# Token mixing rounds: GpSimd instead of VectorE makes the low part of one weight unit per round

## The chip, the cores and the metric

The kernel runs on one core of a Trainium2 chip. The metric is the device time of one execution in microseconds (us), and of several executions the median. The core has TensorE (PE in the profile), VectorE (DVE), ScalarE (ACT), GpSimd (POOL) and SyncE (SP), each with its own queue that is worked off in order. They meet at semaphores. TensorE's weight loads are shown as PEld.

## The reference, cut to what matters

Three layers in a row: a mixing layer (a recurrent branch and a sparse attention branch), a feed-forward layer with 16384 experts, and a second block of two attention-like layers. Only the first is touched, and in it the recurrent branch:

```python
p_rw, q, c_kv, iq, ik, iw, gates = _split(xn @ w_in[l], IN_SPLITS)
y_a = _rwkv7_time_mix(p_rw, ...) @ w_branch_rwkv[l]
y_b = _dsa_attention(q, c_kv, iq, ik, iw, ...) @ w_branch_dsa[l]
g_a, g_b = jnp.split(jax.nn.sigmoid(gates), N_BRANCHES, axis=-1)
h = h + (g_a * y_a + g_b * y_b) @ w_out[l]
...
def step(S, inp):            # inside _rwkv7_time_mix, over 256 tokens
    r_t, k_t, v_t, kk_t, a_t, w_t = inp
    sa = jnp.einsum('bhvk,bhk->bhv', S, -kk_t)
    S = (S * w_t[:, :, None, :] + sa[..., None] * (kk_t * a_t)[:, :, None, :]
         + v_t[..., None] * k_t[:, :, None, :])
    return S, jnp.einsum('bhvk,bhk->bhv', S, r_t)
```

Everything is float32. The recurrence of 16 heads of 64 columns isn't walked token by token in the kernel but in chunks, which needs the inverse of a small triangular matrix for each block of 16 tokens.

## The kernel before, in words

**Weights.** All large weights come in one stream, cut into units of 128 x 2048 float32 (1 MB). A unit passes through one of four slots (`SLOTS`), unit u through slot u % 4: SyncE fetches it into `ring`, ScalarE rounds it to `hi_w` in two halves of 1024 columns (`split_hi`, lines 217 and 218), and another engine makes the rest `lo_w` = `ring` - `hi_w` in two halves (`split_lo`, lines 223 and 225; in this part of the kernel VectorE through the local `lo`). TensorE multiplies three times, hi x hi, lo x hi and hi x lo (line 695, in `quarter`), 24 products of 512 columns for a unit, in four quarters. When it is through with unit u, it raises `unit_used`, and SyncE fetches unit u + 4. So VectorE makes the low part of unit u + 3 while TensorE is at about unit u.

**The block that the change touches** runs 92 units (`LASTU`). Each engine has a loop over them, written out at build time, and between units stand the steps of the other work, at fixed places given as unit and quarter (`due`). The engines other than TensorE number their steps one ahead (`U = u + 1`).

**Token mixing rounds.** There are four rounds n = 0 to 3, each 12 units after the one before: half of the heads (8) for half of the tokens (128). Round n starts at unit 35.25 + 12 n (`RB`, `RSTEP`). Of a round these steps matter here, with their distance in units from the start:

- `steps_out`, `steps_in`: the small triangular blocks go out to DRAM and come back as `Lp` (GpSimd issues the second).
- `off_block` (5.25, line 1549) and **`solve`** (6 to 6.5, lines 1557 to 1562), both on VectorE: `solve` is the forward substitution, 15 times a product `terms` <- `Xs`, `Lp` and a sum over it into `Xs`, with a drain between any two. The last raises `X_ready`.
- `steps_back` on GpSimd waits for `X_ready`, writes `Xs` out to `T_dram` and, when that has landed, reads it back as `TC` (lines 1337, 1342).
- `keys_norm` of the next round (lines 1478 to 1489, with a square root on ScalarE at 1268).
- `spread` (10, line 1571) on VectorE makes `TT` from `TC`; the drain behind it (line 1573) raises `TT_sb`.
- `first` (10.25, line 915) on TensorE waits for `TT_sb`; `second` and `third` (lines 924, 931) follow.

In round 0 VectorE has the token shift of other columns in between (`shift`: lines 1460, 1464, 1468, on `prev` and `RKV`); its first step waits for a transfer that GpSimd issues. In round 3 the three parts of `solve` alternate with `turned_y` (line 1634, one input in PSUM), and behind them in VectorE's queue stands `gated(77)` (line 1646), which reads the products of units 76 and 77 from PSUM and so gives TensorE their bank back for the last two quarters of unit 78. GpSimd has nothing in this block but memsets and transfers; further on in the kernel it does make low parts (line 2076).

In VectorE's queue the low part of unit 44, 56, 68 or 80 (slot 0 each time) stands right behind `solve` in rounds 0 to 2, and behind `gated(77)` in round 3.

Of the kernel before, what the change touches and what calls it, by code (L numbers as in the profile page):

```python
# [19 lines left out]
SLOTS = 4  # L20
# [95 lines left out]
def build(nc, dram, consts):  # L116
# [13 lines left out]
    def S(name):  # L130
        if name not in sems:
            sems[name] = nc.alloc_semaphore(name)
        return sems[name]
# [379 lines left out]
    rows = [slice(CH * c, CH * c + CH) for c in range(NCH)]  # L513
    RB, RSTEP, LASTU, DSAU = 35.25, 12, 92, 36
    LMB = (3, 4, 6, 7)

    def due(u, g, o):

# [22 lines left out]
    with nc.Block() as block:  # L541
# [755 lines left out]
        @block.gpsimd  # L1297
        def _(g):
            def shift(m):

                n = WIDTH.get(m, 512)
                src = zs if m == 4 else part_of(m - 5)
                if m == 4:
                    g.wait_ge(S("iq_T"), 1)
                else:
                    g.wait_ge(S("mixed"), m - 4)
                g.memset(prev[0:1, 0, :], 0.0).then_inc(S("prev_zero"), 1)
                g.wait_ge(S("rkv_in"), m - 3)
                g.dma_start(prev[1:P, :, 0:n], src[0:P - 1, :, 0:n]).then_inc(S("prev_in"), 16)
                g.dma_start(prev[0:1, 1, 0:n], src[P - 1:P, 0, 0:n]).then_inc(S("prev_in"), 16)  # L1310

            def gate_out(c):

                g.wait_ge(S("gate_sb"), c + 1)
                g.dma_start(gates[:, :, c * 512:(c + 1) * 512].rearrange("t p f -> p t f"), gst[:]).then_inc(S("gate_out"), 16)

            def steps_in(n):

                g.wait_ge(S("L_out"), 128 * n + 128)
                if n == 0:  # L1320
                    g.wait_ge(S("z_ps"), 1)
                else:
                    g.wait_ge(S("T_out"), 32 * n)
                g.dma_start(Xs[:], consts["unit_x"].rearrange("p (j t) -> p j t", j=8)).then_inc(S("X0_in"), 16)
                for q in range(2):
                    g.dma_start(Lp[64 * q:64 * q + 64], Ld.rearrange("h b s t -> (h b) s t")).then_inc(S("L_in"), 16)

            def clear(ap, name):
                g.memset(ap[0:64, :, 64:P], 0.0)
                g.memset(ap[64:P, :, 0:64], 0.0)  # L1330
                g.drain().then_inc(S(name), 1)

            def steps_back(n):

                g.wait_ge(S("X_ready"), n + 1)
                for q in range(2):
                    g.dma_start(Td.rearrange("h b s t -> (h b) s t")[:, 8 * q:8 * q + 8, :], Xs[64 * q:64 * q + 64])\
                        .then_inc(S("T_out"), 16)
                g.wait_ge(S("T_out"), 32 * n + 32)
                if n:  # L1340
                    g.wait_ge(S("TT_sb"), n)
                g.dma_start(TC[:], Td.rearrange("h b s t -> h (b s) t").rearrange("h r t -> r h t")).then_inc(S("T_in"), 16)

            def mix_out(c):

                g.wait_ge(S("mb_sb"), c + 1)
                g.dma_start(mixed_dram[:, :, c * 512:(c + 1) * 512].rearrange("t p f -> p t f"), part_of(1 + c % 2))\
                    .then_inc(S(f"mb_out{c % 2}"), 16)

            for u in range(LASTU):  # L1350
                m, q = divmod(u, SLOTS)
                if u == 32:
                    g.wait_ge(S("z_ps"), 1)
                    g.memset(zgT2[32:33, 0, :], 1.0)
                    g.memset(zgT2[64:65, 0, :], 1.0)
                    g.memset(zgT2[32:33, 1, :], 0.0)
                    g.drain().then_inc(S("one_row"), 1)
                for n in range(4):
                    if u == math.ceil(RB + RSTEP * n + 3.6):
                        steps_in(n)  # L1360
                        clear(state_of(n, 1), "K_zero")
                    if u == math.ceil(RB + RSTEP * n + 6.5):
                        steps_back(n)
                if q == 3 and 4 <= m <= 10:
                    shift(m)
                if q == 3 and 11 <= m < 19:
                    gate_out(m - 11)
                if u == 46:
                    g.wait_ge(S("scaled"), 7)
                    clear(ST0[:], "ST0_zero")  # L1370
                if u >= WIN and u < WIN + 8 and (u - WIN) % 2:
                    mix_out((u - WIN) // 2)

        @block.vector
        def _(v):
# [286 lines left out]
            for U in range(1, LASTU + 1):  # L1662
                u = U - 1
                m, q = divmod(u, SLOTS)
                if u == 3:
                    norm_c()
                if u in PAIR:
                    maxima(PAIR[u])
                if u >= WIN and (u - WIN) % 2:
                    gated(u)  # L1670
                if u + 3 < LASTU + 2:
                    lo(u + 3)
                if u in (11, 13):
                    scores((u - 11) // 2)
                if u == 12:
                    top(0, 0, 8)
                    penalty(0)
                if 14 <= u < 18:
                    top(1, 2 * (u - 14), 2)
                if u == 18:  # L1680
                    penalty(1)
                if u in PAIR:
                    scale_p(PAIR[u])
                if 5 <= m <= 11 and q < 3:
                    shift(m - 1, q)
                if u == 74:
                    v.wait_ge(S("o_hi"), 2)
                    v.tensor_tensor(lo_x[:, 0:8], oT[:], hi_x[:, 0:8].bitcast(F32), ALU.subtract)
                    v.drain().then_inc(S("o_lo"), 1)
                for g in range(4):  # L1690
                    if (U, g) == (WIN + 9, 2):
                        turned_y(3)
                    for n in due(U, g, -3):
                        keys_norm(n, 0)
                    for n in due(U, g, -2.5):
                        keys_norm(n, 1)
                    for n in due(U, g, 0.5):
                        rates(n)
                    for n in due(U, g, 1.5):
                        prepare(n)  # L1700
                    for n in due(U, g, 2):
                        ends(n)
                    for n in due(U, g, 2.5):
                        turned_k(n)
                    for n in due(U, g, 3):
                        masked(n, range(4))
                    for n in due(U, g, 3.5):
                        masked(n, range(4, 8))
                    for n in due(U, g, 4):
                        bonus(n)  # L1710
                    for n in late_due(U, g, 15.75, 12.75):
                        center(n)
                    for n in late_due(U, g, 16.25, 13.25):
                        finish(n)
                    for n in due(U, g, 5.25):
                        off_block(n)
                    for k in range(3):
                        for n in due(U, g, 6 + k / 4):
                            solve(n, k)
                    for n in due(U, g, 10):  # L1720
                        spread(n)
                    for n in due(U, g, 10.5):
                        copy4(n, one1, 4, "one_ps", "one_v")
                    for n in due(U, g, 10.75):
                        v.wait_ge(S("two_ps"), n + 1)
                        for q in range(4):
                            tt_(one2[:, 2 * q:2 * q + 2].rearrange("p e (a c) -> p a e c", a=2),
                                PS[:, 5 + q // 2, (q % 2) * 256:(q % 2 + 1) * 256].rearrange("p (e a c) -> p a e c", e=2, a=2),
                                EM[:, q].rearrange("p a (e c) -> p a e c", e=2), ALU.add)
                        v.drain().then_inc(S("two_v"), 1)  # L1730
                        fades(n)
                    for n in due(U, g, 11):
                        copy4(n, WU, 4, "W_ps", "W_v")
                    for n in due(U, g, 11.25):
                        moves(n)
                    if U == WIN + 1 and g:
                        turned_y(g - 1)
# [564 lines left out]
    GU, AU, KU, LASTU = 48, 64, 80, 83  # L2302
# [494 lines left out]
    QU, AU, LASTU = 16, 32, 48  # L2797
# [557 lines left out]
```

## Time and profile before

| what | us |
|---|---|
| median of 3 runs | 3724.7 (3722.67 to 3726.25) |
| the profiled execution | 3719.19 |
| its span from first to last instruction | 3717.4 |
| TensorE busy | 3547.2 (95% of the span) |
| VectorE busy | 2148.9 (58%) |
| ScalarE busy | 1740.7 (47%) |
| GpSimd busy | 345.0 (9%) |

The mean granted clock of TensorE is 0.979 of full speed. How to read the rows further down: a timeline row gives start and duration of an instruction in us from the start of the span, then engine, line, operation, `out<-in`, the shapes, and in brackets for how long the engine had been idle before it and what ended that. A duration in a row of VectorE or GpSimd contains the time for which the instruction was started but held up. A q behind an engine's name means its sequencer (a drain, a semaphore or the issue of a transfer).

### The profile page before, as it was taken

The numbers are of one execution on the slowest core, as the hardware profiler recorded it, in microseconds if no ns is written. First come the engines' busy times: TensorE is split into PE (matmuls) and PEld (weight loads), VectorE is DVE, ScalarE is ACT, GpSimd is POOL, SyncE is SP. The second block draws the span as 40 slices with busy tenths as digits, with TensorE's granted clock in tenths as the row PEclk, the third lists the DMA queues.
The fourth block names the chain that finished last, engine by engine and source line by source line (L and its number), as shares of the span: only waits on it lengthen the run. The fifth ranks groups of instructions, "written<-read, shape, count | busy, mean of one in ns | idle before, by whom it ended". The sixth has DMA issues, their size and how long they took to land. (4 is left out here: it accounts for less than half of the span.)

```text
span 3717.4 us, 50884 instructions
## 1 busy us (share of the span) xinstructions
PE 3547.2 (95%) x20442; PEld 3018.0 (81%) x20442; DVE 2148.9 (58%) x2858; ACT 1740.7 (47%) x2595; POOL 345.0 (9%) x217
## 2 busy tenths in 40 slices
PE   7899999988889999999999999998799999999999
PEld 6677777677779999888899998887688887788777
DVE  4676556644545668655544455554678876465454
ACT  4454333323334478544444444444555544444762
POOL 0001000000039910000000000000022210000000
PEclk9999999899999999999999999999899999999999
DMA  5464234344535555555555565555443434455344
GB/s 209 137 209 146 100 135 150 138 182 160 182 136 181 181 173 177 185 214 192 186 210 182 211 252 189 209 189 192 140 141 139 142 132 182 174 192 193 125 148 159
DMA packets 111179, 638.53 MB, mean 172 GB/s; under 512 B 18506, under 2 KB 24426, under 8 KB 38936
## 3 DMA queue, kind: packets, MB, share of 16 engines
q1 hardware_dynamic: 105128, 621.90, 47.0%
q0 software_dynamic: 5296, 13.15, 1.1%
q8 instruction: 115, 1.88, 0.2%
q10 hardware_dynamic: 576, 1.07, 0.1%
q14 instruction: 64, 0.52, 0.0%
HBM read 611.10 MB, written 21.54 MB: 170 GB/s over the span
## 5 line engine op out<-in xcount | busy, mean ns | idle before, releaser
L223 DVE TENSOR_TENSOR lo_w<-ring,hi_w 128x1024 fp32r<-128x1024 f32 x500 | 612.3, 1225 | 1014.6 <-ACT hi_w L217 1006.6
L217 ACT CAST hi_w<-ring 128x1024 fp32r<-128x1024 f32 x540 | 569.0, 1054 | 989.8 <-DMA ring<-in_wstream 964.8
L225 DVE TENSOR_TENSOR lo_w<-ring,hi_w 128x1024 fp32r<-128x1024 f32 x500 | 611.7, 1223 | 0.0
L1923 PE MATMUL PS<-hi_x,hi_w 128*128 128x256 f32 x2048 | 576.1, 281 | 5.3 <-POOL lo_w L225 2.9
L1923 PE MATMUL PS<-hi_x,lo_w 128*128 128x256 f32 x2048 | 581.1, 284 | 0.0
L1923 PE MATMUL PS<-lo_x,hi_w 128*128 128x256 f32 x2048 | 571.6, 279 | 0.0
L218 ACT CAST hi_w<-ring 128x1024 fp32r<-128x1024 f32 x540 | 564.7, 1046 | 0.0
L1949 PE MATMUL PS<-hi_w,lo_g 128*128 128x512 f32 x1024 | 405.5, 396 | 0.0
L1949 PE MATMUL PS<-hi_w,hi_g 128*128 128x512 f32 x1024 | 401.5, 392 | 1.0 <-issue 1.0
L1949 PE MATMUL PS<-lo_w,hi_g 128*128 128x512 f32 x1024 | 399.4, 390 | 0.0
L1923 PEld LDWEIGHTS PS<-hi_x,hi_w 128*128 128x128 f32 x2048 | 389.9, 190 | 5.9 <-ACT GG L2053 3.2
L1923 PEld LDWEIGHTS PS<-hi_x,lo_w 128*128 128x128 f32 x2048 | 384.9, 188 | 0.0
L1923 PEld LDWEIGHTS PS<-lo_x,hi_w 128*128 128x128 f32 x2048 | 384.7, 188 | 0.0
L695 PE MATMUL PS<-hi_w,hi_x 128*128 128x512 f32 (+2 forms) x736 | 303.1, 412 | 22.9 <-DVE lo_w L225 14.2
L695 PE MATMUL PS<-hi_w,lo_x 128*128 128x512 f32 (+2 forms) x736 | 291.7, 396 | 0.0
L695 PE MATMUL PS<-lo_w,hi_x 128*128 128x512 f32 (+2 forms) x736 | 288.7, 392 | 0.0
L2352 PE MATMUL PS<-hi_w,hi_x 128*128 128x512 f32 x640 | 257.6, 403 | 17.1 <-DVE lo_w L225 9.5
L2352 PE MATMUL PS<-hi_w,lo_x 128*128 128x512 f32 x640 | 254.3, 397 | 0.0
L2352 PE MATMUL PS<-lo_w,hi_x 128*128 128x512 f32 x640 | 250.5, 391 | 0.0
L2053 ACT ACTIVATE GG<-PS 128x256 f32<-128x256 f32 x128 | 81.3, 636 | 337.0 <-PE PS L1923 334.5
L1949 PEld LDWEIGHTS PS<-lo_w,hi_g 128*128 128x128 f32 x1024 | 192.1, 188 | 47.4
L1949 PEld LDWEIGHTS PS<-hi_w,lo_g 128*128 128x128 f32 x1024 | 192.3, 188 | 44.3
(542 smaller groups left out, 5757.6 us busy)
## 6 DMA issues: line engine op xcount, KB each, us to landing
ring<-in_wstream SPq DMA_DIRECT2D x540, 1024.0 KB, 4.8
other_G<-staged SPq DMA_DIRECT2D x32, 256.0 KB, 6.0
hot<-other_G SPq DMA_DIRECT2D x8, 1024.0 KB, 6.8
x<-in_x SPq DMA_DIRECT2D x2, 2048.0 KB, 8.5
gates_dram<-gst POOLq DMA_DIRECT2D x8, 512.0 KB, 4.7
x_dram<-x SPq DMA_DIRECT2D x2, 2048.0 KB, 10.2
x<-x_dram SPq DMA_DIRECT2D x2, 2048.0 KB, 9.1
prev<-RKV POOLq DMA_DIRECT2D x6, 508.0 KB, 5.5
```

What stands on the lines that cost most here:

```text
L217: a.copy(hi_w[s][:, 0:HALF], ring[s][:, 0:HALF]).then_inc(S(f"hi{s}"), 1)
L218: a.copy(hi_w[s][:, HALF:UNIT], ring[s][:, HALF:UNIT]).then_inc(S(f"hi{s}"), 1)
L223: v.tensor_tensor(lo_w[s][:, 0:HALF], ring[s][:, 0:HALF], hi_w[s][:, 0:HALF].bitcast(F32), ALU.subtract)
L225: v.tensor_tensor(lo_w[s][:, HALF:UNIT], ring[s][:, HALF:UNIT], hi_w[s][:, HALF:UNIT].bitcast(F32), ALU.subtract)\
L695: mm = nc.tensor.matmul(PS[:, bank(m, tt), 0:n], xa[:, xo + kk_, tt * P:(tt + 1) * P], wa[slot][:, k * 512:k * 512 + n], start=(kk_ == 0 a ...
L1923: m = nc.tensor.matmul(PS[:, s, 0:T], wa[s][:, k * P:(k + 1) * P], xa[:, k, :], start=(k == 0 and p == 0), stop=(k == KC - 1 and p == 2))
L1949: m = nc.tensor.matmul(PS[:, 4 * tt + c, :], ga[:, s, tt * P:(tt + 1) * P], wa[s][:, c * 512:(c + 1) * 512], start=first and p == 0, stop= ...
L2053: a.activation(gg(i), PS[:, i % SLOTS, 0:T], ACT.Gelu).then_inc(S("gelu_free"), 1)
L2352: mm = nc.tensor.matmul(o, xa[:, kk, tt * P:(tt + 1) * P], wa[q][:, k * 512:(k + 1) * 512], start=(kk == 0 and p == 0), stop=(kk == KC - 1 ...
```

## The change

`LENT` holds one step number per round: int(35.25 + 12 n + 6) = 41, 53, 65, 77. At these steps VectorE leaves out the low part of unit u + 3, which is 44, 56, 68, 80, and GpSimd's loop makes it. The instructions, their operands and their semaphores are the same.

```diff
@@ -513,6 +513,7 @@
     RB, RSTEP, LASTU, DSAU = 35.25, 12, 92, 36
     LMB = (3, 4, 6, 7)
+    LENT = [int(RB + RSTEP * n + 6) for n in range(4)]
@@ -1355,6 +1356,8 @@
                     g.drain().then_inc(S("one_row"), 1)
+                if u in LENT:
+                    split_lo(g, (u + 3) // SLOTS, (u + 3) % SLOTS)
                 for n in range(4):
@@ -1668,7 +1671,7 @@
                     gated(u)
-                if u + 3 < LASTU + 2:
+                if u + 3 < LASTU + 2 and u not in LENT:
                     lo(u + 3)
```

VectorE at the end of `solve` in round 0, before the change (`terms`, `Xs`: the substitution; `prev`, `RKV`: the token shift):

```order
L1560 TENSOR_TENSOR terms_291<-Xs_290,Lp_289 128x128
L1562 TENSOR_REDUCE Xs_290<-terms_291 128x8
L223 TENSOR_TENSOR lo_w0_49<-ring0_53,hi_w0_57 128x1024
L225 TENSOR_TENSOR lo_w0_49<-ring0_53,hi_w0_57 128x1024
L1464 TENSOR_TENSOR prev_248<-prev_248,mixr_247 128x1024
L223 TENSOR_TENSOR lo_w1_50<-ring1_54,hi_w1_58 128x1024
```

And with the change:

```order
L1563 TENSOR_TENSOR terms_291<-Xs_290,Lp_289 128x128
L1565 TENSOR_REDUCE Xs_290<-terms_291 128x8
L1467 TENSOR_TENSOR prev_248<-prev_248,mixr_247 128x1024
L223 TENSOR_TENSOR lo_w1_50<-ring1_54,hi_w1_58 128x1024
L225 TENSOR_TENSOR lo_w1_50<-ring1_54,hi_w1_58 128x1024
```

The two halves of slot 0 are gone from behind the substitution; all other rows keep their order.

GpSimd at the same place, before (the token shift's transfers, then `steps_back`):

```order
L1310 DMA prev_248<-RKV_217 1x16x32
L1337 DMA T_dram<-Xs_290 64x128 x2
L1342 DMA TC_277<-T_dram 128x8x16
L1307 MEMSET prev_248 1x512
```

And with the change:

```order
L1311 DMA prev_248<-RKV_217 1x16x32
L223 ISA
L223 TENSOR_TENSOR lo_w0_49<-ring0_53,hi_w0_57 128x1024
L225 TENSOR_TENSOR lo_w0_49<-ring0_53,hi_w0_57 128x1024
L1338 DMA T_dram<-Xs_290 64x128 x2
L1343 DMA TC_277<-T_dram 128x8x16
L1308 MEMSET prev_248 1x512
```

The two halves now stand ahead of `steps_back`; the configuring instruction (`ISA`), which stood ahead of GpSimd's first low part much further on, moves here with them.

VectorE in round 3, before, behind the last product of `solve`:

```order
L1634 TENSOR_TENSOR lo_x_62<-PS,hi_x_64 128x4x128
L1646 TENSOR_TENSOR RKV_217<-PS,RKV_217 128x512 x2
L223 TENSOR_TENSOR lo_w0_49<-ring0_53,hi_w0_57 128x1024
L225 TENSOR_TENSOR lo_w0_49<-ring0_53,hi_w0_57 128x1024
L223 TENSOR_TENSOR lo_w1_50<-ring1_54,hi_w1_58 128x1024
```

And with the change:

```order
L1637 TENSOR_TENSOR lo_x_62<-PS,hi_x_64 128x4x128
L1649 TENSOR_TENSOR RKV_217<-PS,RKV_217 128x512 x2
L223 TENSOR_TENSOR lo_w1_50<-ring1_54,hi_w1_58 128x1024
L225 TENSOR_TENSOR lo_w1_50<-ring1_54,hi_w1_58 128x1024
```

Here the two halves are gone from behind `gated(77)`.

## Rows read from the trace of the kernel before

**Rows 1.** TensorE's waits, 330 to 790 us: total, times, longest.

```profile
PE PS L915 <- DVEq L1573: 12.9, 4, 4.7
PE PS L695 <- DVE RKV L1646: 8.7, 1, 8.7
```

**Rows 2.** Timelines of ScalarE and GpSimd where the latter makes low parts.

```profile
1066.32 1.05 ACT L217 CAST hi_w<-ring 128x1024 fp32r<-128x1024 f32 x1
...
1067.45 2.36 POOL L223 TENSOR_TENSOR lo_w<-ring,hi_w 128x1024 fp32r<-128x1024 f32 x1 [269.14 <-ACT hi_w L217]
...
1129.99 2.41 POOL L225 TENSOR_TENSOR lo_w<-ring,hi_w 128x1024 fp32r<-128x1024 f32 x1
1133.29 2.41 POOL L223 TENSOR_TENSOR lo_w<-ring,hi_w 128x1024 fp32r<-128x1024 f32 x1 [0.89 <-ACT hi_w L217]
1135.66 4.47 POOL L225 TENSOR_TENSOR lo_w<-ring,hi_w 128x1024 fp32r<-128x1024 f32 x1
```

**Rows 3.** Timeline of VectorE in the same time.

```profile
1131.44 1.11 DVE L2157 TENSOR_TENSOR route<-tops 128x128 f32<-128x128 f32 x1
...
1133.47 4.38 DVE L2165 TENSOR_TENSOR hot<-ppf,iota 128x2048 f32<-128x2048 f32 x1
```

**Rows 4.** One VectorE line beside GpSimd's work: ns min/median/max, first and last start.

```profile
L2660 DVE TENSOR_TENSOR AM<-AM x32: 424/426/2207, 2715.2 to 3080.4; 128x256 f32<-128x256 f32 x32
```

**Rows 5.** Timelines of ScalarE, VectorE and TensorE, round 0.

```profile
349.79 1.05 ACT L217 CAST hi_w<-ring 128x1024 fp32r<-128x1024 f32 x1 [4.66 <-DMA ring<-in_wstream]
...
351.11 1.23 DVE L1460 TENSOR_TENSOR prev<-prev,RKV 128x1024 f32<-128x1024 f32 x1 [4.54 <-DMA prev<-RKV]
...
352.45 0.18 DVE L1560 TENSOR_TENSOR terms<-Xs,Lp 128x16 f32<-128x16 f32 x1
...
362.79 1.22 DVE L223 TENSOR_TENSOR lo_w<-ring,hi_w 128x1024 fp32r<-128x1024 f32 x1
...
365.24 1.23 DVE L1464 TENSOR_TENSOR prev<-prev,mixr 128x1024 f32<-128x1024 f32 x1
...
379.69 1.22 DVE L1571 TENSOR_TENSOR TT<-TC,blockm 128x1024 f32<-128x1024 f32 x1
...
365.21 0.80 PE L695 MATMUL PS<-hi_w,hi_x 128*128 128x512 f32 x1 [4.78 <-DVE lo_w L225]
...
380.99 3.65 PE L915 MATMUL PS<-EM,TT 128*128 128x128 f32 x16 [4.65 <-DVEq L1573]
```

**Rows 6.** Timelines of ScalarE and VectorE, round 1.

```profile
478.89 1.05 ACT L217 CAST hi_w<-ring 128x1024 fp32r<-128x1024 f32 x1 [4.34 <-DMA ring<-in_wstream]
...
480.34 0.29 DVE L1560 TENSOR_TENSOR terms<-Xs,Lp 128x72 f32<-128x72 f32 x1
...
481.01 0.30 DVE L1560 TENSOR_TENSOR terms<-Xs,Lp 128x80 f32<-128x80 f32 x1
...
486.35 1.23 DVE L223 TENSOR_TENSOR lo_w<-ring,hi_w 128x1024 fp32r<-128x1024 f32 x1
...
492.28 1.23 DVE L223 TENSOR_TENSOR lo_w<-ring,hi_w 128x1024 fp32r<-128x1024 f32 x1 [1.29 <-ACT hi_w L217]
```

**Rows 7.** Timelines of VectorE and GpSimd, round 2.

```profile
609.46 1.23 DVE L223 TENSOR_TENSOR lo_w<-ring,hi_w 128x1024 fp32r<-128x1024 f32 x1 [0.99 <-ACT hi_w L217]
...
617.62 1.22 DVE L1571 TENSOR_TENSOR TT<-TC,blockm 128x1024 f32<-128x1024 f32 x1
...
610.14 0.93 POOL L1342 DMA_DIRECT2D TC<-T_dram  x1 [5.03 <-DMA T_dram<-Xs]
```

**Rows 8.** Timelines of ScalarE, VectorE and TensorE, round 3.

```profile
714.37 1.05 ACT L217 CAST hi_w<-ring 128x1024 fp32r<-128x1024 f32 x1 [0.47 <-DMA ring<-in_wstream]
...
716.21 0.23 DVE L1560 TENSOR_TENSOR terms<-Xs,Lp 128x40 f32<-128x40 f32 x1
...
727.54 0.79 PE L695 MATMUL PS<-hi_w,hi_x 128*128 128x512 f32 x1 [8.69 <-DVE RKV L1646]
...
738.47 1.29 DVE L1646 TENSOR_TENSOR RKV<-PS,RKV 128x512 f32<-128x512 f32 x2 [5.61 <-PE PS L695]
```

## The prediction, as it was put on record

> **What bounds the kernel now.** I looked first at TensorE's waits in the stretch of the token mixing rounds [rows 1]. TensorE is busy for 95% of the whole span, so a change on another engine can only bring what it takes from such waits, and can cost what it adds to them. Three waits touch the change. TensorE waits four times for the drain behind `spread`, 12.9 us in all: each round's chain over `solve` and `spread` is late. It waits once, 8.7 us, for `gated(77)`, which stands behind `solve` in round 3. And it waits once, 4.78 us, for the low part of a weight unit [rows 5]: that is unit 44, the unit that the change moves in round 0. Then I read the timelines of the four rounds [rows 5 to 8], and at last the place where GpSimd already makes low parts, for what that costs the two engines [rows 2 to 4].
>
> **What the change takes away.** On VectorE it removes two instructions of 1.22 us per round; from the start of the first to the start of what follows it is 365.24 - 362.79 = 2.45 us in round 0; in round 1 two low parts in a row take 492.28 - 1.29 - 486.35 = 4.64 us, so 2.32 each [rows 5, 6]. What that is worth depends on what VectorE meets next:
> - Round 0: behind the low part VectorE has work without a gap up to `spread` at 379.69 (its only idle bits are 0.3 us for a square root that itself waits for VectorE), and TensorE waits for it until 380.99, after a wait of 4.65 us. So 2.45 us come off the end. The wait of 4.78 us for unit 44's low part goes too, but this is worth nothing by itself: TensorE would only arrive earlier at `first`, and wait longer there.
> - Round 1: two units on, VectorE is idle for 1.29 us until ScalarE has the high part of unit 58 [rows 6], which in turn waits for TensorE's progress. Worth 0.
> - Round 2: the same with 0.99 us [rows 7]. Worth 0.
> - Round 3: the low part stood behind `gated(77)`; the next thing in VectorE's queue that matters is idle for 5.61 us before it [rows 8]. Worth 0.
>
> If nothing else happened, the change would bring 2.45 us.
>
> **What the change adds.** GpSimd gets two instructions. Left alone they take 2.36 to 2.41 us each [rows 2], some 4.8 us together, and start 0.08 us after ScalarE's first half (1067.45 against 1066.32 + 1.05 in rows 2). In round 0 that is 350.84 + 0.08 = 350.92 us, in round 1 480.02, in round 3 715.50 [rows 5, 6, 8]. TensorE wants unit 44 from 365.21 - 4.78 = 360.4 us on, so GpSimd is in time even if each half takes 4.47 us, as one in rows 2 does (350.92 + 8.94 = 359.9). But in every round this falls right into `solve`, and there the two engines meet.
>
> Rows 2 and 3 show how. VectorE's product at 1131.44, of only 128 elements, takes 1.11 us and ends 0.15 us after GpSimd's 1129.99 + 2.41 = 1132.40. The one at 1133.47 started under a GpSimd instruction that ends at 1135.70, and takes 4.38 us, and GpSimd's next one, from 1135.66, takes 4.47 us and ends 2.28 us after VectorE's end at 1137.85. So they don't slow each other a little: one waits until the other's whole instruction is over, and who stands waiting gets the next turn, also between two GpSimd instructions that follow each other. Line 2660 says the same over 32 instructions: 424 ns at the least, 2207 ns where GpSimd has one of its own [rows 4]. All of these VectorE instructions read two tensors in SBUF, and so do `shift` and the products of `solve`. The sums of `solve` read one; I take them to run freely, in the gaps.
>
> The Trainium skill has this as a rule that speaks against the change ("SBUF — State Buffer", section "Who interferes with whom"): a VectorE instruction with two inputs in SBUF and a GpSimd instruction that reads SBUF shut each other out for the length of a whole instruction, and it is the order of issue that decides who waits. The rows above agree; without the rule and the rows the sum would be the bare gain of the part before.
>
> By that I go through the rounds:
> - Round 0. GpSimd starts at 350.92, VectorE's `shift` was started at 351.11. It waits until 353.27 (2.35 us for GpSimd's half) and ends some 1.1 us later, at 354.37. GpSimd's second half ends 2.28 us behind that, at 356.65. The first product of `solve`, which ended at 352.45 + 0.18 = 352.63, ends just after, at 356.75. Loss 4.12 us, less 2.45: **1.67 us** later at `spread` and `first`.
> - Round 1. GpSimd from 480.02 to 482.37. The product of 480.34, done at 480.63 before, is done at 482.45; the second half follows until 484.75, and the product that was done at 481.31 is done at 484.85. Loss 3.54 us. VectorE had 2.32 us of removed work and 1.29 us of idle time before unit 58's low part, 3.61 us together: **0**.
> - Round 2. The same loss of about 3.55 us, against 2.32 + 0.99 = 3.31 us: **0.25 us**.
> - Round 3. GpSimd from 715.50 to 717.85. The product of 716.21, done at 716.44 before, has another ahead of it that is held up until 717.92; GpSimd's second half then ends at 720.20 and this product at 720.29. Loss 3.85 us. This all goes to `gated(77)`, since VectorE had no idle time before it, and TensorE is waiting: it starts again at 731.4 in place of 727.54. The removed low part stood behind it. **3.85 us**.
>
> Sum: 1.67 + 0 + 0.25 + 3.85 = **5.8 us slower**. The profiled execution's span of 3717.4 us would be 3723.2; that execution stood at 3719.19, 5.5 us under the median of 3724.7, so I put the same difference on the median: **3730.5 us**.
>
> Nearest rows on both sides: if the small products were not held up at all, the sum is -2.45; if each round paid both GpSimd instructions in full (2 x 2.41 = 4.8 us), it is 2.35 + 1.2 + 1.5 + 4.8 = 9.85. I take the values between, since the row of 128 elements at 1131.44 is like those of `solve` (16 to 128 elements).
>
> Costed at nothing: the configuring instruction, which no row of a timeline shows. It runs while GpSimd is idle, in front of its wait for ScalarE; if it took some us, GpSimd would start later, still inside `solve`, and have 3.7 us to spare before TensorE wants unit 44. Behind the two new instructions stands `steps_back`, which waits for `X_ready`: in all rounds GpSimd is done before `solve` is, so it starts no later than `X_ready`, and this is later by the loss. In round 2 the read was issued at 610.14, when the write had landed, and `spread` came at 617.62 [rows 7]; 3.6 us later the read is issued at 613.7 and has 4 us left.
>
> **The rivals.**
> (a) *Nothing is held up.* The small products slip through, and round 0 gains its 2.45 us: 3722.3 us. For it: rows 3 and 4 show no instruction as small, and with drains between, as those of `solve`. Against it: 1131.44, with 128 elements. Were GpSimd to lose every race and VectorE none, it would end the same.
> (b) *GpSimd keeps its turn over both halves.* The gap between its two instructions is nothing, and a small product that waits might not get in between. Then a block of 4.7 us stands in one piece: 4.3 us lost in round 0 (1.9 net), 4.2 in rounds 1 and 2 (0.6 and 0.9 net), 4.35 in round 3: 7.8 us, 3732.5 us, slower by just over 0.2%. For it: the missing gap. Against it: at 1135.66 VectorE did get in between.
> (c) *The substitution's result comes back too late.* GpSimd waited 5.03 us for the write to `T_dram` in round 2 [rows 7], while weights were on their way too. Shifted by 3.6 us in rounds 1 and 2, write and read may each catch the next 1 MB of weights. I can only estimate it: if the read lands over 4 us after its issue, each us more goes to `spread`; with 5 to 5.5 us, as the write took, `spread` comes 1 to 1.5 us later in both: 5.8 + 2.7 = 8.5, 3733.2 us, slower.
> (d) *The change does not do what it says*: the rows of the order show that it does, so this has no share.
>
> **How the numbers follow.** 3730.5 us is +0.16%, and 0.2% (7.4 us) is about what a measurement of this kernel can tell from no change, so my forecast is on the edge between no difference and a small loss. Chances: the forecast 0.62, (a) 0.10, (b) 0.13, (c) 0.10, anything else 0.05. (b) and (c) are slower by more than 0.2%, of the forecast itself about a seventh falls beyond it by noise: slower 0.30. A gain over 7.4 us needs a thing that I don't see: faster 0.03. The rest, 0.67, is no difference. The range leaves out (a) and a little on the upper side: 3726.5 to 3734.
>
> **What would show it.** In the profile of the changed kernel, GpSimd has four pairs at about 350.9, 480, 596.7 and 715.5 us (the later ones shifted by what came before), the first halves 2.4 us and the second ones 2.4 to 3.5 us long. In each `solve` exactly two instructions of VectorE take some 2 us (in round 0 one is `shift`). TensorE's wait for unit 44 is gone and stands before unit 45; the wait for `gated(77)` is some 12.5 us instead of 8.69; the wait for `spread` in round 0 is longer than 4.65. It would be wrong if the products of `solve` have their old durations, or if the block of rounds ends more than 8 us later.

## The result, and the profile after

| | before | changed |
|---|---|---|
| median of 20 runs each, us | 3725.26 (3715.34 to 3728.17) | 3731.84 (3726.11 to 3737.85) |
| ratio, 95% interval | | 1.0023 [1.0016, 1.0029] |
| span of the profiled execution, us | 3717.4 | 3732.4 |
| mean granted clock in it | 0.979 | 0.976 |

The changed kernel is slower, by 6 to 11 us after the interval. The medians lie 6.6 us apart, the ratio says 8.6 us. Within 0.2% or beyond it is on the edge, as forecast. The two profiled executions lie 15 us apart, and that is not the size of the change. From `shift` in round 0 to `first` in round 3 the changed one takes 9.4 us longer, and 3 of these come from a stretch in which TensorE ran at a lower granted clock (last section); some 6 more arise behind `first` of round 3, where nothing was changed. A single pair of traces is read for mechanisms here, the ratio for the size.

TensorE's waits in the changed kernel, 330 to 790 us (who waited for whom: total, times, longest), to be read beside [rows 1]:

```profile
PE PS L916 <- DVEq L1576: 18.1, 4, 8.6
PE PS L696 <- DVE RKV L1649: 12.8, 1, 12.8
...
PE PS L696 <- DVE lo_w L225: 5.0, 1, 5.0
```

The waits for `spread` grew from 12.9 to 18.1 us, the one for `gated(77)` from 8.7 to 12.8. The wait for a low part is still there; it is now the one for unit 45.

Round 0, GpSimd and VectorE in the changed kernel (start and duration in us; answers to [rows 5]):

```profile
349.31 2.40 POOL L223 TENSOR_TENSOR lo_w<-ring,hi_w 128x1024 fp32r<-128x1024 f32 x1 [5.46 <-ACT hi_w L217]
351.68 3.39 POOL L225 TENSOR_TENSOR lo_w<-ring,hi_w 128x1024 fp32r<-128x1024 f32 x1
...
350.44 2.36 DVE L1463 TENSOR_TENSOR prev<-prev,RKV 128x1024 f32<-128x1024 f32 x1 [5.68 <-DMA prev<-RKV]
352.76 0.07 DVE L1560 MEMSET Lp<- 128x16 f32 x1
352.92 2.18 DVE L1563 TENSOR_TENSOR terms<-Xs,Lp 128x16 f32<-128x16 f32 x1
355.18 0.17 DVE L1565 TENSOR_REDUCE Xs<-terms 128x8 f32<-128x16 f32 x1
355.43 0.18 DVE L1563 TENSOR_TENSOR terms<-Xs,Lp 128x24 f32<-128x24 f32 x1
```

One can follow the turns. GpSimd's first half ends at 351.71; VectorE's `shift`, started at 350.44, ends 1.1 us after that, at 352.80, and has taken 2.36 us in place of 1.23. GpSimd's second half was started at 351.68, waits for it, and ends at 355.07. The first product of the substitution, 16 elements wide, takes 2.18 us in place of 0.18 and ends 0.03 us later. The next one is back at 0.18.

Round 3, GpSimd, VectorE and TensorE (answers to [rows 8]):

```profile
720.52 2.39 POOL L223 TENSOR_TENSOR lo_w<-ring,hi_w 128x1024 fp32r<-128x1024 f32 x1 [8.90 <-ACT hi_w L217]
722.87 2.37 POOL L225 TENSOR_TENSOR lo_w<-ring,hi_w 128x1024 fp32r<-128x1024 f32 x1
...
720.52 2.43 DVE L1563 TENSOR_TENSOR terms<-Xs,Lp 128x24 f32<-128x24 f32 x1
723.02 0.18 DVE L1565 TENSOR_REDUCE Xs<-terms 128x8 f32<-128x24 f32 x1
723.28 2.03 DVE L1563 TENSOR_TENSOR terms<-Xs,Lp 128x32 f32<-128x32 f32 x1
725.38 0.19 DVE L1565 TENSOR_REDUCE Xs<-terms 128x8 f32<-128x32 f32 x1
725.65 0.23 DVE L1563 TENSOR_TENSOR terms<-Xs,Lp 128x40 f32<-128x40 f32 x1
...
736.98 0.79 PE L696 MATMUL PS<-hi_w,hi_x 128*128 128x512 f32 x1 [12.77 <-DVE RKV L1649]
```

Two products are held up. The sum between them, with one input in SBUF, is not: it starts at 723.02, under GpSimd's second half, and takes 0.18 us. TensorE waits 12.77 us for its bank.

Read from the starts and ends in the traces, in us (`solve` from the memset of `Lp` to the end of the last sum):

| | before | changed | changed, second trace |
|---|---|---|---|
| `solve`, round 0 / 1 / 2 / 3 | 10.4 / 10.1 / 10.3 / 11.3 | 12.4 / 13.7 / 13.7 / 15.4 | 12.4 / 13.8 / 14.1 / 15.0 |
| round 0, from the start of `shift` (line 1460, at 351.11 before) to `first` | 29.9 | 32.7 | 32.9 |
| TensorE's wait for `spread`, rounds 1 / 2 | 3.43 / 3.43 | 4.08 / 4.06 | 4.11 / 4.03 |
| its wait for `gated(77)` | 8.69 | 12.77 | 12.42 |

### The profile page after: what moved, and what is told of

Read it like the earlier page. It is cut to its first block and busy times, and to the rows that moved or that the text cites. A ratio compares the mean times of both kernels' runs of the same rounds, so it can differ in the third digit from the quotient of the medians.

```text
span 3732.4 us, 50884 instructions
## 1 busy us (share of the span) xinstructions
PE 3552.8 (95%) x20442; PEld 3023.4 (81%) x20442; DVE 2156.3 (58%) x2850; ACT 1740.4 (47%) x2595; POOL 365.7 (10%) x225
```

## The experiments

Theory **H**: VectorE instructions with two inputs in SBUF and GpSimd instructions that read SBUF exclude each other for a whole instruction, and this is the loss. Rivals: **C**, most of it is granted clock; **P**, the place in GpSimd's queue costs, not the reading; **F**, rounds 0 to 2 hide a further loss; and for round 0 **D** against **E**, below.

### The changed kernel again

No edit.

> The changed kernel once more, beside the others on the same chip. Theory H (hold-up: a VectorE instruction that reads two SBUF tensors and a GpSimd instruction that reads SBUF exclude each other for a whole instruction): 5 to 10 us slower than before, six substitution products and one shift of VectorE stretched to about 2 us each, as in the first trace of the changed kernel. Theory C (the loss is for its larger part a lower granted clock of TensorE that happened to lie in those executions, such as at 640 to 655 us): the same stretched instructions, but the loss between executions moves with the granted clock, and the dip at 640 us is missing in this trace.

Measured: 3734.85 us, ratio 1.0025 [1.0015, 1.0034]; the same waits and the same stretched instructions (third column above). The dip of the clock at 640 us is missing in this trace (granted clock 1.00 from 640 to 656 us, and 0.57 in the first), and the ratio is the same. So the loss is not that dip, and the mechanism repeats. C falls for the whole of the loss, but the clock is not out of it. Its mean over the executions is 0.9765 (20) and 0.9762 (10) in the changed kernel, 0.9779 (32) in the kernel before and 0.9777 (11) in the kernel with zeros of the next part, which has no stretched product. As an estimate, 0.0015 less over 3725 us is 11 us more at the lower of the two levels, which is half speed. A good part of that is TensorE's longer waits themselves: in the one for `gated(77)` the granted clock is 0.50 (727 to 735 us in the first trace). How much slower work around the waits adds is not separated.

### GpSimd writes zeros and reads nothing

This kernel leaves out the low part of four units' weights.

```diff
+    def blank_lo(g, k, s):
+        g.wait_ge(S(f"hi{s}"), k * 2 + 1)
+        g.memset(lo_w[s][:, 0:HALF].bitcast(F32), 0.0)
+        g.wait_ge(S(f"hi{s}"), k * 2 + 2)
+        g.memset(lo_w[s][:, HALF:UNIT].bitcast(F32), 0.0).then_inc(S(f"lo{s}"), 1)
...
-                    split_lo(g, (u + 3) // SLOTS, (u + 3) % SLOTS)
+                    blank_lo(g, (u + 3) // SLOTS, (u + 3) % SLOTS)
```

> GpSimd writes zeros into the low parts of units 44, 56, 68 and 80 at the same places, in two memsets that read nothing (so this part of the products is left out: the low part of four units of weights counts as zero). H: no product of the substitution is stretched, VectorE is free of its two instructions at no price, round 0 gains its 2.4 us and round 3 starts again at its old distance: 2 to 3 us faster than before, that is 8 to 11 us faster than the changed kernel. Rival P (it is the place in GpSimd's queue or in the semaphores that costs, not the reading): as slow as the changed kernel.

Measured: 3722.07 us, ratio 0.9997 [0.9988, 1.0006]. Timelines of GpSimd, VectorE and TensorE in this kernel:

```profile
349.11 0.97 POOL L231 MEMSET lo_w<- 128x1024 f32 x1 [5.20 <-ACT hi_w L217]
350.05 0.96 POOL L233 MEMSET lo_w<- 128x1024 f32 x1
...
349.40 1.23 DVE L1470 TENSOR_TENSOR prev<-prev,RKV 128x1024 f32<-128x1024 f32 x1 [5.00 <-DMA prev<-RKV]
350.59 0.07 DVE L1567 MEMSET Lp<- 128x16 f32 x1
350.74 0.18 DVE L1570 TENSOR_TENSOR terms<-Xs,Lp 128x16 f32<-128x16 f32 x1
...
725.03 0.80 PE L703 MATMUL PS<-hi_w,hi_x 128*128 128x512 f32 x1 [8.73 <-DVE RKV L1656]
```

VectorE's `shift` runs through both memsets in its old 1.23 us, the product after it in 0.18, and the wait for `gated(77)` is back at 8.73. The place in the queue and the semaphores are the same as in the changed kernel, so P falls: what GpSimd's instruction does is the cause. The memsets are also shorter (0.96 us against 2.4), but length alone is not it: were VectorE shut out for as long as a memset runs, `shift`, started at 349.40, would have had to wait until 350.08. The memset differs from the subtraction in two things, it reads nothing and it is another operation; no run separates these, so the reading itself is inferred. The gain of 2.4 us in round 0 that H expected is not there: from `shift` to `first` it takes 29.3 us, only 0.6 less than before, and VectorE waits 1.70 us for the token shift's rows ahead of `spread`. That was the first sign of a second effect in round 0. The total, 2 to 3 us faster by H, is not told from no change.

### Only round 3, and only rounds 0 to 2, each twice

```diff
-    LENT = [int(RB + RSTEP * n + 6) for n in range(4)]
+    LENT = [int(RB + RSTEP * n + 6) for n in (3,)]
```

(and with `range(3)` for the other).

> Only the unit of round 3 (80) is moved to GpSimd. H by the sum on record: 3.85 us slower than before, with the wait for gated(77) at 12.5 us instead of 8.69; rounds 0 to 2 as before. C: the wait is longer, but the total is within 2 us of before.

> Only the units of rounds 0, 1 and 2 (44, 56, 68) are moved. H by the sum on record: 1.67 + 0 + 0.25 = 1.9 us slower than before; together with the run in which only round 3 is moved this makes the loss of the changed kernel. C: no difference that the total shows.

Measured: round 3 alone 1.0006 [0.9997, 1.0015], rounds 0 to 2 alone 1.0020 [1.0011, 1.0029]. The wait for `gated(77)` is 12.28 us in the first and 8.73 in the second, as H says. But the ratios are the other way round from H's sum, so both were run again:

> The run with rounds 0 to 2 alone once more, since its interval (4 to 11 us slower) hardly holds what its trace gives: 2.8 us in round 0 and 0.6 us each in rounds 1 and 2, 4.0 us in all (1.0011). Theory H with D: the ratio of both measurements together comes to 1.001 to 1.0015. Theory F (a further loss of 3 us lies in these rounds that the waits don't show): 1.002 again.

> The run with round 3 alone once more, for the same comparison. H: 3.6 to 4.1 us slower than before, 1.001. F: under 1.0006, so that rounds 0 to 2 carry the larger part of the whole loss.

Measured: rounds 0 to 2 alone 1.0006 [0.9997, 1.0015], round 3 alone 1.0007 [0.9998, 1.0016], its wait 12.77 us. Both pairs taken together: 1.0013 and 1.0007, some 4.8 and 2.4 us, in sum 7.2, against 8.6 for the whole. F is not borne out: the two measurements of rounds 0 to 2 differ as their mean granted clock does, 0.9766 at 1.0020 and 0.9775 at 1.0006. But the intervals of these small differences are 3 us to either side, and both for round 3 alone include no change, so the split between the rounds rests on the waits in the traces and not on the ratios. For the same reason the totals do not decide between H and C for round 3.

### Half the work on GpSimd

GpSimd makes the first half of each of the four units, VectorE the second at its old place.

```diff
-                    split_lo(g, (u + 3) // SLOTS, (u + 3) % SLOTS)
+                    k, s = divmod(u + 3, SLOTS)
+                    g.wait_ge(S(f"hi{s}"), k * 2 + 1)
+                    g.tensor_tensor(lo_w[s][:, 0:HALF], ring[s][:, 0:HALF], hi_w[s][:, 0:HALF].bitcast(F32), ALU.subtract)\
+                        .then_inc(S("half_lo"), 1)
...
+                    v.wait_ge(S(f"hi{s}"), k * 2 + 2)
+                    v.wait_ge(S("half_lo"), LENT.index(u) + 1)
+                    v.tensor_tensor(lo_w[s][:, HALF:UNIT], ring[s][:, HALF:UNIT], hi_w[s][:, HALF:UNIT].bitcast(F32), ALU.subtract)\
+                        .then_inc(S(f"lo{s}"), 1)
```

> GpSimd makes only the first half of the low parts of units 44, 56, 68 and 80, VectorE the second at its old place. H: one instruction of VectorE is stretched in each `solve` and not two: rounds 1 and 2 take 11.9 us for it (10.05 before, 13.7 in the changed kernel), and TensorE's wait for gated(77) is 10.6 us (8.69 before, 12.5 in the changed kernel). If a meeting of the two engines cost a fixed amount instead, `solve` would be as long as in the changed kernel.

Measured: a single execution, 3726.57 us, which says nothing on the total. `solve` takes 12.03 us in rounds 1 and 2 (in round 0 it is `shift` that is held up, and `solve` keeps its 10.4), and TensorE, in its timeline:

```profile
733.28 0.79 PE L696 MATMUL PS<-hi_w,hi_x 128*128 128x512 f32 x1 [10.93 <-DVE RKV L1652]
```

11.9 and 10.6 us were expected. The price goes by the instruction of GpSimd: some 2 us of VectorE for each (2.0 and 1.8 us here, 3.4 to 4.1 for two in rounds 1 to 3 of the table above).

### The token shift's rows in round 0

VectorE's and SyncE's timelines of the changed kernel in round 0:

```profile
380.72 1.23 DVE L1463 TENSOR_TENSOR prev<-prev,RKV 128x1024 f32<-128x1024 f32 x1 [1.97 <-DMA prev<-RKV]
...
366.63 0.33 SPq L561 DMA_DIRECT2D mixr<-in_shift_mix  x1
367.01 0.94 SPq L633 DMA_DIRECT2D ring<-in_wstream  x2
```

And SyncE's before the change:

```profile
366.52 0.33 SPq L560 DMA_DIRECT2D mixr<-in_shift_mix  x1
366.90 7.01 SPq L632 DMA_DIRECT2D ring<-in_wstream  x2
```

VectorE now waits 1.97 us for the token shift's rows, just ahead of `spread`; before it did not. In the rows of SyncE the second column is from the first issue to the end of the second: two weight units (47 and 48) go out within 0.94 us, and before the second went out 6.7 us after the first. The cause is the wait that the change removed. SyncE stands until about 366.5 us at a semaphore of the token shift in both kernels; TensorE is now already through with unit 44 by then, so that both slots are free and 2 MB of weights are issued at once, ahead of the token shift's 0.5 MB. From issue to landing, in us (last column; 508 KB and 2 KB), before and then changed:

```profile
prev<-RKV POOLq DMA_DIRECT2D x1, 508.0 KB, 4.2
prev<-RKV POOLq DMA_DIRECT2D x1, 2.0 KB, 4.9
...
prev<-RKV POOLq DMA_DIRECT2D x1, 508.0 KB, 8.0
prev<-RKV POOLq DMA_DIRECT2D x1, 2.0 KB, 9.1
```

To test it:

```diff
                 sp.wait_ge(S("unit_used"), u + 1)
+                if u == 44:
+                    sp.wait_ge(S("prev_in"), 224)
                 sp.dma_start(ring[u % SLOTS][:], wst[u + SLOTS]).then_inc(S(f"landed{u % SLOTS}"), 16)
```

> The changed kernel, and SyncE issues the transfer of weight unit 48 only when the token shift's transfer of round 0 has landed (it waits for prev_in). Theory D (in round 0 the changed kernel frees unit 44 earlier, so that two 1 MB weight transfers are issued at once ahead of the token shift's rows, which then land 2 us late for VectorE): the rows land about 5 us after their issue and not 9, VectorE doesn't wait for them, `spread` comes 7.0 us after the start of the next round's `keys_norm` as before the change, and not 9.1. Rival E (the wait comes from GpSimd, which issues the rows late): still 9 us. The total is for this single look not told from the changed kernel's.

Measured: a single execution, 3728.83 us. The rows land after 4.9 and 5.6 us, and VectorE reaches `shift` and `spread` without a gap:

```profile
379.19 1.22 DVE L225 TENSOR_TENSOR lo_w<-ring,hi_w 128x1024 fp32r<-128x1024 f32 x1
380.32 1.22 DVE L1465 TENSOR_TENSOR prev<-prev,RKV 128x1024 f32<-128x1024 f32 x1
381.46 1.22 DVE L1576 TENSOR_TENSOR TT<-TC,blockm 128x1024 f32<-128x1024 f32 x1
```

From `keys_norm` to `spread` it takes 7.0 us, as before the change, and 9.1 in the changed kernel. D is shown; E falls, since GpSimd issues the rows 1.8 us ahead of `keys_norm` in both kernels. From `shift` to `first` it takes 30.6 us here, against 29.9 before and 32.7 in the changed kernel: of the loss in round 0 some 2.1 us are the late rows, and only 0.7 is what the hold-up costs beyond the work taken from VectorE.

### The low part behind `spread`

If H holds, GpSimd should work where VectorE waits. In every round VectorE is idle from the end of `spread` until TensorE is through `first`, and right ahead of `spread` stands the low part of a unit that TensorE wants only after that (47, 59, 71, 83).

```diff
-    LENT = [int(RB + RSTEP * n + 6) for n in range(4)]
+    LENT = [int(RB + RSTEP * n + 9) for n in range(4)]
...
                 if u in LENT:
+                    g.wait_ge(S("TT_sb"), LENT.index(u) + 1)
                     split_lo(g, (u + 3) // SLOTS, (u + 3) % SLOTS)
...
                     g.wait_ge(S("scaled"), 7)
+                    g.drain()
                     clear(ST0[:], "ST0_zero")
```

(The drain stands ahead of a memset further on in GpSimd's loop, in all three kernels of this part.)

> In each round GpSimd makes the low part three units later: units 47, 59, 71 and 83, which on VectorE stand right ahead of `spread`; and it starts only when `spread` is done (it waits for TT_sb), where VectorE is idle until TensorE is through `first`. H: VectorE is held up by little, `spread` comes 2.3 us earlier in rounds 0 to 2 and 1.3 us in round 3: about 8 us faster than before (3717 against 3725). Rival L (a unit made so late is late for TensorE, or the hold-up hits what VectorE does behind `first`): no gain, and TensorE waits for this low part.

Measured: 3716.06 us against 3722.54, ratio 0.9982 [0.9973, 0.9991], faster than both kernels. Round 1, VectorE, GpSimd and TensorE:

```profile
498.56 1.22 DVE L1576 TENSOR_TENSOR TT<-TC,blockm 128x1024 f32<-128x1024 f32 x1
501.95 0.69 DVE L1583 COPY one<-PS 128x512 f32<-128x512 f32 x1 [2.17 <-PE PS L916]
503.51 2.18 DVE L223 TENSOR_TENSOR lo_w<-ring,hi_w 128x1024 fp32r<-128x1024 f32 x1 [0.87 <-ACT hi_w L217]
...
499.89 2.35 POOL L223 TENSOR_TENSOR lo_w<-ring,hi_w 128x1024 fp32r<-128x1024 f32 x1 [5.24 <-DVEq L1578]
502.22 2.39 POOL L225 TENSOR_TENSOR lo_w<-ring,hi_w 128x1024 fp32r<-128x1024 f32 x1
...
499.86 1.38 PE L916 MATMUL PS<-EM,TT 128*128 128x128 f32 x10 [1.16 <-DVEq L1578]
```

TensorE's wait for `spread` in round 1 is 1.16 us in place of 3.43 (2.27 less; the same in round 2). In round 0 the way from `keys_norm` to `first` is only 1.5 us shorter (6.80 in place of 8.33 us), since VectorE waits 0.66 us for the token shift's rows. One meeting is left, behind the gap: VectorE's low part at 503.51 takes 2.18 us. Rival L has that much for it: TensorE now waits 1.76 us at `third` in round 1, where it had not waited. But `third` starts 8.4 us behind `first`, against 9.3 us before, so nothing of the gain is lost there.

Without the wait for `TT_sb` (and with the drain):

> As the run behind `spread`, but without the wait for TT_sb: GpSimd starts as soon as ScalarE's first half is there, under the square root step and `spread`, which both read SBUF twice or wait behind such. H: `spread` is held up by one GpSimd instruction or two, about what the removed low part gives back: within 2 us of before in rounds 0 to 2, so 5 to 8 us slower than the run with the wait. Rival L: as fast as the run with the wait or faster, since GpSimd is done earlier.

Measured: 3722.04 us, ratio 0.9998 [0.9989, 1.0007]. Round 1, VectorE and GpSimd:

```profile
505.65 3.37 DVE L1575 TENSOR_TENSOR TT<-TC,blockm 128x1024 f32<-128x1024 f32 x1
...
505.51 2.42 POOL L223 TENSOR_TENSOR lo_w<-ring,hi_w 128x1024 fp32r<-128x1024 f32 x1 [3.51 <-ACT hi_w L217]
507.90 3.33 POOL L225 TENSOR_TENSOR lo_w<-ring,hi_w 128x1024 fp32r<-128x1024 f32 x1
```

`spread` is started when GpSimd is 0.14 us into its first half and takes 3.37 us in place of 1.22: what the removed low part gives is taken back at once. GpSimd starts earlier than in the run with the wait, and by the medians the kernel is 6 us slower than that one.

With SyncE's wait as well:

> The kernel with the low part behind `spread`, and the same wait of SyncE. D: in round 0 VectorE's last 0.8 us of waiting for the token shift's rows goes too, so 3716 us less at most 1, not to be told from the run without it; 7 to 9 us faster than before. E: the same as without it.

Measured: 3712.80 us against 3724.02, ratio 0.9973 [0.9963, 0.9984], the fastest. In round 0 it takes 6.54 us from `keys_norm` to `first`, and 6.80 without SyncE's wait: that wait is worth 0.3 us here. The intervals of the two ratios overlap, so the two are not told apart.

## Why the prediction was right, point by point

- **What bounds the stretch** was right: the waits for `spread` in rounds 0 to 2, the one for `gated(77)` and the one for unit 44 are where the change acts. The wait for `spread` in round 3 stays as it was (1.34 us before, 1.35 and 1.44 in the changed kernel).
- **The two engines exclude each other**: right, down to the turns. In each of the eight meetings with GpSimd in each trace of the changed kernel, one VectorE instruction takes some 2 us (`shift` 1.1 to 1.3 us more than alone). Rival (a), nothing is held up, fell. Rival (b), GpSimd keeps its turn over both halves, fell too: in round 0 `shift` got in between, and in round 3 the product of 720.52. That it is the reading of GpSimd's instruction is the one part that no run isolates.
- **Round 3**: 3.85 us predicted; the wait grew by 3.6 to 4.1 us in the five traces that have this move, alone or with the others (12.77, 12.42, 12.28, 12.77 and 12.33 us).
- **Rounds 1 and 2**: 0 and 0.25 us predicted, 0.6 to 0.7 each in TensorE's wait for `spread` in the two traces (0.4 to 1.0 over all with this move). `solve` grew by 3.5 to 3.8 us in place of 3.54, and in round 1 it started some 0.3 us later against TensorE. The slack of 3.6 and 3.3 us had been taken at its full size; from the end of `solve` to `spread` only 3.3 and 3.4 us were given back in round 1, and 2.8 and 3.1 in round 2. Two terms that nearly cancel were given to 0.05 us, though the single durations vary by 0.2.
- **Round 0**: 1.67 us predicted, 2.8 to 3.0 found. The term that failed is "behind the low part VectorE has work without a gap up to `spread`". The loss itself was smaller than 4.12 us (3.2 from `shift` to the end of `solve` in the first trace, 3.4 in the second), since GpSimd had started 1.1 and 0.9 us ahead of `shift` and not the 0.19 us that the prediction took from the trace before. The 2.45 us came back, but the token shift's rows now landed 2.0 us too late. The prediction had dismissed the vanished wait for unit 44 with "worth nothing by itself"; it had a price, since it freed a slot earlier and so moved 1 MB of weights ahead of a transfer that VectorE needs.
- **Rival (c)**, a result of the substitution that comes back too late, named the right kind of thing (a transfer behind the weights), and the larger case of it was another transfer, the token shift's rows. In small it came true as well. The prediction had given the read of `TC` 4 us to spare; in round 2 of the first trace it was issued at 615.39, and `spread` waited 0.51 us for it (the row below). In the second trace it waited 0.20 us in round 1, before the change in no round. The sum had put this at nothing.

```profile
619.45 1.23 DVE L1574 TENSOR_TENSOR TT<-TC,blockm 128x1024 f32<-128x1024 f32 x1 [0.51 <-DMA TC<-T_dram]
```

- **The sum**: 5.8 us predicted. From the traces it is 2.9 + 0.65 + 0.6 + 3.9, some 8 us, and the ratio says 8.6 [6, 11], so the forecast stands at the lower end. The predicted 3730.5 is 1.3 us from the measured median, and that is partly luck: in round 0 a hold-up put 0.7 to 1.0 us too high made up for a part of the 2 us of late rows that the sum did not have, and the two medians lie only 6.6 us apart.
- **One sign of being wrong did show**: the block of rounds was to end at most 8 us later. TensorE's last wait near its end (5.05 us, up to 807.93 before) ends at 817.89 and 820.18 in the two traces of the changed kernel, 10 and 12 us later. It was a poor sign for a single pair of traces: `shift` in round 0, ahead of the first meeting, starts anywhere from 349.4 to 355.9 us in the thirteen traces.

## What to carry to other kernels

Work handed from VectorE to GpSimd has to be placed against what VectorE does at that moment, not only against its total load. Here each subtraction of GpSimd that met a VectorE instruction with two inputs in SBUF cost VectorE 1 to 2.2 us. The chain of small products was the worst place of those tried (8.6 us slower), and the idle stretch behind `spread` the best (6.7 us faster than before), though GpSimd had to be made to wait for it. And when a wait disappears, ask what its end had been holding back: here it was a 1 MB transfer on another engine's queue.

## What the runs showed of the hardware that I had not expected

A product of 16 elements costs VectorE 2.18 us when it meets a subtraction on GpSimd, and 0.18 us when it meets none; a GpSimd memset over 1024 columns costs `shift` nothing. The exclusion thus hits the shortest instructions by the largest factor, here twelvefold.

Executions of one kernel differ by 12 to 18 us, and part of this is TensorE's granted clock in stretches that differ from one execution to the next. Over all executions on record, a mean granted clock lower by 0.001 goes with a time some 3 us longer within one kernel. Windows 640 to 656 us (length, busy of each engine, PEclk, DMA), before and then changed:

```profile
640.00:648.00 8.00, 8.00 (x100) 5.75 (x100) 1.20 (x2) 0.73 (x2) 0.00 (x0) 1.00 0.13 32
648.00:656.00 8.00, 8.00 (x82) 4.83 (x79) 0.00 (x0) 0.73 (x2) 0.00 (x0) 0.88 0.24 101
...
640.00:648.00 8.00, 8.00 (x36) 6.04 (x34) 2.36 (x2) 2.08 (x3) 0.00 (x0) 0.59 0.01 2
648.00:656.00 8.00, 8.00 (x67) 5.72 (x68) 0.00 (x0) 0.73 (x2) 0.00 (x0) 0.55 0.15 37
```

Between its small products (lines 949 to 986) TensorE ran at the lower of its two levels (1.2 GHz, 0.5 in the profile) for most of 16 us in the changed kernel's trace, and mostly at the higher (2.4 GHz) in the other. In the 15 us before, it had been busy in both (14.3 and 14.9 us) at a granted clock of 1.00. It fell 6 us behind in the dip, and won back 3 of them by the wait for `gated(77)`, since the trace before has a low stretch of its own from 656 us on (0.83 to 680 us, against 0.93). The second trace of the changed kernel has no such dip there. What starts it is left open.
